# Attention scores three items ahead, and the copies of transposed probabilities on alternating engines

## The reference, cut to what matters

```python
DILATED_PATTERNS = ((128, 1), (512, 4), (2048, 16))
scores = jnp.where(mask, q @ k * (e ** -0.5), -jnp.inf)   # band of +- window/(2*dilation)
lse = logsumexp(scores); p = exp(scores - lse); o = p @ v
attn = sum(softmax(lses)[i] * outs[i])                    # over the patterns
```

## Time and profile before

| | |
|---|---|
| median of 3 runs | 3775.27 us |
| profiled execution | 3779.01 us |
| its span (first to last instruction) | 3776.9 us |
| TensorE matmul busy | 3500.8 us (93%) |
| VectorE, ScalarE, GpSimd busy | 2375.9, 1825.3, 443.7 us |
| mean granted TensorE clock | 0.957 |

### The profile page before, as it was taken

How to read it: one execution, slowest core, us unless ns; L and a number is a source line. 1 busy time by engine, 2 the same in 40 slices (tenths; PEclk the granted TensorE clock), 3 DMA queues, 4 the chain that set the end, 5 groups by cost and what they waited for, 6 DMA issues and landing times. The chain is left out here.

```text
span 3776.9 us, 62068 instructions
## 1 busy us (share of the span) xinstructions
PE 3500.8 (93%) x20174; PEld 3095.5 (82%) x20174; DVE 2375.9 (63%) x3941; ACT 1825.3 (48%) x3108; POOL 443.7 (12%) x399
## 2 busy tenths in 40 slices
PE   8999698785993999999999999999999999999993
PEld 6888688573552989989899898998989989899993
DVE  6421166785556767767666676676766767667674
ACT  3222266110111655656555565565655656556564
POOL 0010154332330000000000000000000000000002
PEclk9999899796995999999999999999999999999997
DMA  4221333112223777767777777777777777777775
GB/s 161 78 65 68 75 79 91 38 37 100 103 94 107 227 238 234 232 224 234 237 237 215 234 232 234 234 231 221 234 237 236 225 236 234 220 234 223 238 234 186
DMA packets 238871, 689.07 MB, mean 182 GB/s; under 512 B 52608, under 2 KB 68768, under 8 KB 238400
## 3 DMA queue, kind: packets, MB, share of 16 engines
q1 hardware_dynamic: 222240, 628.47, 52.1%
q0 software_dynamic: 15552, 54.72, 5.3%
q10 hardware_dynamic: 864, 3.15, 0.2%
HBM read 635.81 MB, written 50.43 MB: 182 GB/s over the span
## 5 line engine op out<-in xcount | busy, mean ns | idle before, releaser
L1751 PE MATMUL moe_gu<-moe_xgT,moe_whi 128*128 128x384 f32 x5632 | 1632.6, 363 | 7.3 <-issue 3.4
L1883 DVE TENSOR_TENSOR moe_wlo<-moe_raw,moe_whi 128x1024 fp32r<-128x1024 f32 x1056 | 1290.3, 1223 | 480.4 <-ACT moe_whi L1837 475.7
L1752 PE MATMUL moe_gu<-moe_xgT,moe_wlo 128*128 128x192 f32 x5632 | 1413.4, 251 | 0.0
L1837 ACT CAST moe_whi<-moe_raw 128x1024 fp32r<-128x1024 f32 x1056 | 1105.9, 1048 | 441.4 <-PE moe_dnp L1767 389.1
L1752 PEld LDWEIGHTS moe_gu<-moe_xgT,moe_wlo 128*128 128x128 f32 x5632 | 1083.1, 192 | 0.4
L1751 PEld LDWEIGHTS moe_gu<-moe_xgT,moe_whi 128*128 128x128 f32 x5632 | 1064.3, 189 | 12.6 <-issue 4.7
L1844 ACT COPY moe_part<-moe_gu 128x384 f32<-128x384 f32 x352 | 168.7, 479 | 461.1 <-PE moe_gu L1752 440.6
L1889 DVE TENSOR_TENSOR moe_guv<-moe_gu,moe_part 128x384 f32<-128x384 f32 x352 | 196.1, 557 | 288.7 <-ACT moe_part L1844 288.6
L1716 POOL DMA_INDIRECT tmp_acc<-moe_og_s,moe_srow_s x16 | 29.1, 1816 | 2273.1 <-ACT moe_og_s L1869 1409.7
L1763 PE MATMUL moe_dns<-moe_whi,moe_hid 128*128 128x512 f32 x704 | 276.0, 392 | 0.0
L1766 PE MATMUL moe_dnp<-moe_whi,moe_hid 128*128 128x512 f32 x704 | 275.7, 392 | 0.0
(11 more groups left out here) (269 smaller groups left out, 4073.1 us busy)
## 6 DMA issues: line engine op xcount, KB each, us to landing
moe_raw<-in_w_ffn SPq DMA_DIRECT2D x1056, 512.0 KB, 4.1
prj_wraw<-in_w_in SPq DMA_DIRECT2D x12, 1024.0 KB, 5.4
att_raw<-tmp_qkT SPq DMA_DIRECT2D x32, 384.0 KB, 6.9
prj_share<-in_xT SPq DMA_DIRECT2D x6, 1024.0 KB, 10.5
tmp_qkT<-prj_share POOLq DMA_DIRECT2D x24, 256.0 KB, 2.7
ssd_xb<-tmp_xbc SPq DMA_DIRECT2D x12, 512.0 KB, 3.9
mix_xr<-in_x SPq DMA_DIRECT2D x12, 512.0 KB, 3.7
tmp_h<-mix_h POOLq DMA_DIRECT2D x12, 512.0 KB, 3.0
```

The costliest lines, as they stand in the source:

```text
L1751: pe.matmul(out[:, a, 0:2 * CAP], whi[c][:, j, :], x, start=(j == 0), stop=False)
L1752: mm = pe.matmul(out[:, a, 0:CAP], wlo[c][:, j, :], x[:, 0:CAP], start=False, stop=(j == KD - 1))
L1837: act.copy(whi[c][:], raw[c][:]).then_inc(hi_done, 1)
L1883: dve.tensor_tensor(wlo[c][:], raw[c][:], whi[c][:].bitcast(F32), ALU.subtract).then_inc(lo_done, 1)
```

## The change

Scores, masks and exponentials run three items ahead in place of two (`AHEAD`), with four buffers of `sc`, `neg` and `probs` (`DEEP`) in place of two. `trA` and `trB` become one tile `tr` (two buffers, all transposes of an item in one), so that the PSUM tiles are again eight: four `sc`, two `tr`, two `o`. The copy from `tr` to `pT` is done by one engine for a whole item: VectorE for even items, ScalarE for odd ones, 384 columns in a narrow item and 512 in a wide one. `copied[b]` takes the place of `copyA` and `copyB`. The diff, cut where lines only rename or repeat:

```diff
+    AHEAD = 3
+    DEEP = AHEAD + 1
...
-        neg = [m.sb(f"neg{s}", [P, 2, WIN]) for s in range(2)]
-        probs = [m.sb(f"probs{s}", [P, 2, WIN]) for s in range(2)]
-        pT = [m.sb(f"pT{s}", [P, 2, 2, P]) for s in range(2)]
-        sc = [m.ps(f"sc{s}", [P, 2, WIN]) for s in range(2)]
-        trA = [m.ps(f"trA{s}", [P, 4, P]) for s in range(2)]
-        trB = [m.ps(f"trB{s}", [P, 4, P]) for s in range(2)]
+        neg = [m.sb(f"neg{s}", [P, 2, WIN]) for s in range(DEEP)]
+        probs = [m.sb(f"probs{s}", [P, 2, WIN]) for s in range(DEEP)]
+        pT = [m.sb(f"pT{s}", [P, 4, P]) for s in range(2)]
+        sc = [m.ps(f"sc{s}", [P, 2, WIN]) for s in range(DEEP)]
+        tr = [m.ps(f"tr{s}", [P, 4, P]) for s in range(2)]
...
             def transposes(h, j):
                 n = ITEMS * h + j
-                b = j % 2
-                pe.wait_ge(exp_done, 2 + n + 1)
-                pe.wait_ge(copyA, n + 1)
-                pe.wait_ge(copyB, n + 1)
-                for i in range(2):
-                    pe.transpose(trA[b][:, i, :], probs[b][:, 0, P * i:P * i + P], ident[:])
-                for i in range(classes(j)[2]):
-                    mm = pe.transpose(trB[b][:, i, :], probs[b][:, 1, P * i:P * i + P], ident[:])
+                b, d = j % 2, n % DEEP
+                pe.wait_ge(exp_done, DEEP + n + 1)
+                pe.wait_ge(copied[b], n // 2 + 1)
+                for i in range(2 + classes(j)[2]):
+                    mm = pe.transpose(tr[b][:, i, :], probs[d][:, i // 2, P * (i % 2):P * (i % 2) + P], ident[:])
                 mm.then_inc(tr_mm, 1)
 
             def values(h, hh, s, j):
...
-                pe.wait_ge(copyA, 2 + n + 1)
-                pe.wait_ge(copyB, 2 + n + 1)
+                pe.wait_ge(copied[b], n // 2 + 2)
...
             def body(h, hh, s, last):
                 for j in range(ITEMS):
-                    if j + 2 < ITEMS:
-                        scores(h, hh, s, j + 2)
+                    if j + AHEAD < ITEMS:
+                        scores(h, hh, s, j + AHEAD)
                     elif not last:
-                        scores(h + 1, hh + s, 1 - s, j + 2 - ITEMS)
+                        scores(h + 1, hh + s, 1 - s, j + AHEAD - ITEMS)
...
-            def copy_half(h, j):
+            def copy_even(h, j):
                 n = ITEMS * h + j
-                b = j % 2
-                dve.wait_ge(tr_mm, 2 + n + 1)
-                dve.wait_ge(pv_mm, PV0 - 2 + n + 1)
-                dve.tensor_copy(pT[b][:, 0], trA[b][:, 0:2, :]).then_inc(copyA, 1)
+                if j % 2 == 0:
+                    tiles = 2 + classes(j)[2]
+                    dve.wait_ge(tr_mm, DEEP + n + 1)
+                    dve.wait_ge(pv_mm, PV0 - 2 + n + 1)
+                    dve.tensor_copy(pT[0][:, 0:tiles, :], tr[0][:, 0:tiles, :]).then_inc(copied[0], 1)
...
-            def copy_half(h, j):
+            def copy_odd(h, j):
                 n = ITEMS * h + j
-                b, nb = j % 2, classes(j)[2]
-                act.wait_ge(tr_mm, 2 + n + 1)
-                act.wait_ge(pv_mm, PV0 - 2 + n + 1)
-                act.copy(pT[b][:, 1, 0:nb, :], trB[b][:, 0:nb, :]).then_inc(copyB, 1)
+                if j % 2:
+                    tiles = 2 + classes(j)[2]
+                    act.wait_ge(tr_mm, DEEP + n + 1)
+                    act.wait_ge(pv_mm, PV0 - 2 + n + 1)
+                    act.copy(pT[1][:, 0:tiles, :], tr[1][:, 0:tiles, :]).then_inc(copied[1], 1)
```

More of the change, by code:

```diff
@@ L495, in stage_attend @@
         tr_mm = m.sem("tr_mm")
-        copyA = m.sem("copyA")
-        copyB = m.sem("copyB")
+        copied = m.sems("copied")
         pv_mm = m.sem("pv_mm")
@@ L551, in _ @@
                              att[:, 1, j, :]).then_inc(comb_out, 16)
-            sp.wait_ge(exp_done, 2 + ITEMS * HEADS)
+            sp.wait_ge(exp_done, DEEP + ITEMS * HEADS)
             for g in range(TOK // GRP):
@@ L592, in _ @@
         def _(pe):
-            pe.sem_inc(tr_mm, 2)
+            pe.sem_inc(tr_mm, DEEP)
             pe.sem_inc(pv_mm, PV0)
@@ L597, in scores @@
                 n = ITEMS * h + j
-                b = j % 2
+                b = n % DEEP
                 if j == 0:
@@ L626, in values @@
                     pe.wait_ge(v_in[s], V_LOADS * (hh + 1))
-                pe.wait_ge(copyA, 2 + n + 1)
-                pe.wait_ge(copyB, 2 + n + 1)
+                pe.wait_ge(copied[b], n // 2 + 2)
                 pe.wait_ge(taken, n + 1)
                 for i in range(2):
-                    pe.matmul(o[b][:, 0:HD], pT[b][:, 0, i, :], vn[s][:, j + i, :], start=(i == 0), stop=(i == 1))
+                    pe.matmul(o[b][:, 0:HD], pT[b][:, i, :], vn[s][:, j + i, :], start=(i == 0), stop=(i == 1))
                 nb, c = classes(j)[2], j % CLS
@@ L634, in values @@
                     tile = c if nb == 1 else CLS + CLS * i + c
-                    mm = pe.matmul(o[b][:, HD:2 * HD], pT[b][:, 1, i, :], vc[s][:, tile, :], start=(i == 0), stop=(i == nb - 1))
+                    mm = pe.matmul(o[b][:, HD:2 * HD], pT[b][:, 2 + i, :], vc[s][:, tile, :], start=(i == 0), stop=(i == nb - 1))
                 mm.then_inc(pv_mm, 1)
@@ L651, in _ @@
             pe.wait_ge(pads, 6)
-            scores(0, 0, 0, 0)
-            scores(0, 0, 0, 1)
+            for j in range(AHEAD):
+                scores(0, 0, 0, j)
             transposes(0, 0)
@@ L658, in _ @@
         def _(dve):
-            dve.sem_inc(masked, 2)
-            dve.sem_inc(copyA, 2)
+            dve.sem_inc(masked, DEEP)
+            dve.sem_inc(copied[0], 1)
             dve.sem_inc(taken, 2)
@@ L689, in body @@
                 for j in range(ITEMS):
-                    if j + 2 < ITEMS:
-                        mask_scores(h, j + 2)
+                    if j + AHEAD < ITEMS:
+                        mask_scores(h, j + AHEAD)
                     elif not last:
-                        mask_scores(h + 1, j + 2 - ITEMS)
+                        mask_scores(h + 1, j + AHEAD - ITEMS)
                     if j + 1 < ITEMS:
-                        copy_half(h, j + 1)
+                        copy_even(h, j + 1)
                     elif not last:
-                        copy_half(h + 1, 0)
+                        copy_even(h + 1, 0)
                     take(h, j)
@@ L705, in _ @@
             dve.tensor_copy(qc[0][:], by_class(q2[0][:])).then_inc(split_done, 1)
-            mask_scores(0, 0)
-            mask_scores(0, 1)
-            copy_half(0, 0)
+            for j in range(AHEAD):
+                mask_scores(0, j)
+            copy_even(0, 0)
             heads(dve, body)
@@ L712, in _ @@
         def _(act):
-            act.sem_inc(exp_done, 2)
-            act.sem_inc(copyB, 2)
+            act.sem_inc(exp_done, DEEP)
+            act.sem_inc(copied[1], 1)
             def exponent(h, j):
                 n = ITEMS * h + j
-                b = j % 2
-                act.wait_ge(masked, 2 + n + 1)
+                b = n % DEEP
+                act.wait_ge(masked, DEEP + n + 1)
                 act.wait_ge(tr_mm, n + 1)
@@ L736, in body @@
                     if j + 1 < ITEMS:
-                        copy_half(h, j + 1)
+                        copy_odd(h, j + 1)
+                    if j + AHEAD < ITEMS:
+                        exponent(h, j + AHEAD)
                     elif not last:
[L739 to L743, removed]
+                        exponent(h + 1, j + AHEAD - ITEMS)
             act.wait_ge(split_done, 2 * SPLITS)
@@ L748, in _ @@
             act.copy(k2[0][:, :, KR:KR + RUN], by_class(raw[0][:, 1, :])).then_inc(split_done, 1)
-            exponent(0, 0)
-            exponent(0, 1)
-            copy_half(0, 0)
+            for j in range(AHEAD):
+                exponent(0, j)
             heads(act, body)
```

## The result

The changed kernel takes 3737.14 us (median of 4 runs, 3733.98 to 3743.55) against 3775.6 us before (the three runs that the forecast had, and a fourth); the ratio is 0.9901, 95% interval 0.9884 to 0.9919. The forecast was 3745.9, in a range of 3737 to 3761: the right direction, 29.4 us forecast and 38.5 measured. The measured time lies 9 us under the forecast, outside its own range of 3741 to 3750, and just inside the lower edge of the wide one. The profiled execution took 3734.54 us, with a span of 3732.7 against 3776.9.

The account below looks back on a forecast made before the run. Latency was taken to bound the attention, a chain of 4.22 us over two items. Savings of 3.8 (head 0), 20.6 (heads 1 to 6) and 5.0 (head 7) make 29.4 us: 3775.27 to 3745.9, range 3737 to 3761, its own 3741 to 3750.

Parts of the forecast that it names:

- TensorE alone sets the pace: Rival, attention: no wait for GpSimd's split, six heads save 1.13 us more each, 36 us in all, 3739; 8%.
- The chain of 4.22 us over two items: Attention: scores, mask, exponentials, transposes take 4.22 us over two items, 2.11 an item; three ahead gives 1.41, no longer a bound.
- half of it: Rival, attention: small waits stay in the loop, 1.95 us per item for 1.77, 20 us saved, 3755; 22%.
- nothing moves: Rival, attention: another latency, for instance copies that the values wait for, takes the chain's place; 3775; 8%.
- TensorE's 1.77 us for a wide item: Attention: scores 0.35, step to transposes 0.14, transposes 0.38, values 0.90 us; a head's own work 19.88 us against 24.4.
- The copies: Copies of 512 columns take 0.68 us on VectorE, at most 0.74 on ScalarE; even copies have 0.29 us to spare.
- the prediction's signs: Trace signs named beforehand, among them VectorE copies of 512 columns near 0.68 us, six a head, and ScalarE's under 0.74.
- The split as next bound: GpSimd's 15.20 us split is ready at 15.81; TensorE waits 1.13 us at loop 9, making heads 21.01 us.
- the rival that VectorE shuts GpSimd out: Rival, attention: denser VectorE work makes GpSimd's split stand aside, heads 31 us, kernel 31 us slower, 3806; 4%.
- The attention's sum: Saving in the attention: head 0 3.8 us, heads 1 to 6 20.6, head 7 5.0, in all 29.4 us.
- The following stages ... cost the same: Stages after the attention start earlier by the 29.4 us saved and cost the same as before.
- The slower rival: Rival, attention: VectorE shuts GpSimd out of its split; slower than before once the split exceeds 20.1 us; 3806; 4%.

Follow-up runs that it names:

- both fillings: Changed kernel with two semaphore increments without a waiter per even item on ScalarE and per odd item on VectorE, meant to restore old program lengths: 3745.9 us.
- the earlier split: Changed kernel with GpSimd's split waiting for the scores of the head two before, not its values: 3730.0 us, against 3733.0 unaltered beside it.

## Why the prediction was right, and where it was not

The range held, but by luck at its edge. By its number the result lies nearest the rival "TensorE alone sets the pace" (3739), and that rival is refuted: the wait for the split stands in all six heads. The forecast was right on the attention, to 0.6 us, and left out 9 us elsewhere.

**The chain of 4.22 us over two items**: right. Run three ahead it vanished, and with two ahead it came back at 4.21. That also answers the rivals "half of it" and "nothing moves": neither transposes nor values wait in a head any more, but for 0.6 us once.

**TensorE's 1.77 us for a wide item**: 1.80. The step from scores to transposes was 0.14 as halved from the earlier trace rows (512.71 to 512.85), but four transposes take 0.42 where they follow without a wait, not 0.38; in the earlier trace rows they came after one. Narrow items took 1.43 to 1.48 for 1.43.

**The copies**: 686 ns forecast as 0.68, ScalarE's 586 under the bound of 0.74; neither holds TensorE, and all copies on one engine give the same heads. Of the six even copies of a head that the prediction's signs give 512 columns, four have them and two have 384 (32 and 16 in the stage); the sum doesn't use the number.

**The split as next bound**: right, and the most useful step. Heads come 20.92 us apart for 21.01 worked out. The wait is 0.74 for 1.13, mostly because TensorE's own loops 0 to 8 take 15.0 us for 14.68, and since the scores start 0.05 us after the split's end (562.13 to 562.18) where 0.20 was allowed. Without the wait heads are 20.18 us, not 19.88. The split lasted 15.27 us for 15.20 beside a denser VectorE, so the rival that VectorE shuts GpSimd out is refuted for this kernel.

**The attention's sum**: 29.4 forecast, 30.0 measured, and the parts hold too. Head 0 gave 4.0 for 3.8 (its end at 484.07 for 488.07), heads 1 to 6 gave 21.1 for 20.6, head 7 gave 4.9 for 5.0. It holds for two traces in which the clock rose equally early (466.4 and 465.2); in four traces of altered forms of the changed kernel it rose 5 to 9 us later, which took up to 4 us back.

**"The following stages ... cost the same"** is the step that failed, by 9 us. The prediction took the later stages at no difference, without a reason. The runs showed in its place that with 96 instructions fewer on VectorE in the attention the experts stage takes 2440.1 us for 2455.8: there are 40 packets of q14 in it for 71, and VectorE is not late where a pass of the experts' loop begins. That the loop now lies where it loads code less often is my reading of the packets. With VectorE's program filled to its old length the time is 3746.8, with both fillings 3745.9 (3743.1 to 3748.6), the forecast; that it agrees to the last digit is chance. Which position is good I could not have read from the rows that I had; a difference in program length was in the diff and I gave it no bound.

**The slower rival** was the wrong mechanism with the right place. A longer split is indeed paid in full, and with 3.1 us more in it the attention took 200.1 us, as long as before (199.9). But nothing shut GpSimd out; the dear part is the clock: a wait of 3.6 us cost a further 3.3 to 4.4 us, in half of the heads. With the change as it is the wait is 0.74 us and the clock stays at 1.00.

What stays open: why 96 added instructions on VectorE bring the loads back and 144 do not. A position of the loop against a block of loaded code would do it, but no run measured such a block; all that the traces show is that nearly all packets of q14 have 8192 bytes.

## What to carry to other kernels

Where every item waits a little for the same engine, write down the chain from scores to scores and divide by the items it spans: that quotient, not a busy share, is the period, and one item more of look-ahead pays until the busiest engine's own sum is reached. Then take the helper engine's preparation of the next block as a loop of its own, with its start condition; it is the next bound, and the earliest true condition (last reader, not last user) may remove it. And give any change that adds or removes instructions ahead of a long loop a term of its own (here 10 to 15 us in a loop of 2450), and compare the instruction queues' packet counts before crediting a gain to the edit.

## What the runs showed of the hardware that I had not expected

The number of instructions on VectorE ahead of a loop changed how often the loop loaded instructions and how late VectorE came at the start of a pass, and not monotonically: with 0, 96 and 144 added there were 65, 96 and 66 packets on the instruction queue q14, and only with 96 was VectorE late (up to 2.4 us). The stage took 2440.1, 2450.8 and 2446.6 us; of the last, the clock explains the excess over 2440.

Three waits of TensorE of 3.6 us were each followed by 14 to 17 us at the lower clock level, although TensorE was busy again at once; waits of 0.7 to 1.7 us were not. And at the start of the stage, after 27 us without work, the clock rose between 464 and 467 us in nine traces and between 470 and 475 in five others of nearly the same program, worth up to 4 us of the whole time; so 3 us between two versions of this kernel, as with the earlier split, need more runs than these.
